# A two-block transformer kernel: the 107 KB scratch arena is allocated after the small constant tensors instead of before them

## The chip, the cores and the metric

The kernel runs on one core of one Trainium2 chip. The time is that of the device in microseconds (us), lower is better. On-chip memory (SBUF) has 128 partitions; a tensor of shape [128, n] takes 4n bytes at the same byte address of each partition when its elements are 32 bits wide. All the addresses below are such addresses inside a partition. They are those of the built program, not something the profile shows.

## The reference

Two blocks run one after the other on 512 tokens of width 1024, all in float32.

```python
def reference(x, ...):
    x = first_block(x, ...)     # DEPTH = 2 layers: w_in, differential attention, gated linear
                                # recurrence (chunk_scan, forward and backward), merge, SwiGLU
    return second_block(x, ...) # 1 layer: sliding-window attention, S5 state space, gated merge,
                                # squared-relu feed-forward

for layer in range(DEPTH):                       # first_block
    h = rmsnorm(x, attn_norm[layer])
    proj = h @ w_in[layer]
    y_a = diff_attention(...) @ w_a[layer]
    y_b = hgrn2_bidirectional(...) @ w_b[layer]
    merged = sigmoid(gate_a) * y_a + sigmoid(gate_b) * y_b
    x = x + merged @ w_o[layer]
    h = rmsnorm(x, ffn_norm[layer])
    x = x + (silu(h @ w_gate[layer]) * (h @ w_up[layer])) @ w_down[layer]
```

## The kernel before

The activations are held transposed in `xT` (feature on the partition, token along it). Every large product is made of three matmuls, because each operand is split into a high part of type fp32r and the remainder: `triple` (lines 355 to 358) multiplies high by high, high by low and low by high into the same accumulator. The weights come in units of 1 MB: the sync engine (SP) loads one into one of the two halves of `raw` (L343), ScalarE (ACT) rounds it into `w_hi` (L349), GpSimd (POOL) subtracts it into `w_lo` (L2652), and TensorE (PE) multiplies. All of this passes in a ring of two halves, guarded by semaphores that are written out by hand. There is no scheduler and no planner: each engine runs its instructions in the order of the code, and waits on semaphores.

A unit is used in one of two ways. In most stages (`pe_feature`, `pe_branch`, `pe_part`) the 128 x 128 weight tile is stationary and a row of 512 tokens of the activation moves: `h_hi`, `o_hi`, `m_hi`, `hid_hi`, `zz_hi` and their low parts. In `pe_token` and in the last product of the second block a 128 x 128 piece of the activation is stationary and 512 columns of the weight move. In the profile's names of a matmul the moving operand stands first: `psG<-hid_hi,w_hi` moves `hid_hi` over a stationary `w_hi`.

The memory of a partition is laid out once, at the top of `build_in`. Tensors made by `sb(...)` are given the next free address, each start rounded up to a multiple of 32 bytes. First come `xT`, `h_hi`, `h_lo`, `raw`, `w_hi` and `w_lo`, 16 KB each. Then comes a block of 107 KB called `arena`, which no instruction uses under its own name. Its start is kept in `base`, and some 90 tensors are placed inside it by hand with `at(name, kb, shape)`, at `base + kb * KB`; several of them share the same bytes at different times. Most intermediate results are there: `x_tok` (the input rows as loaded), `QQ`, `Kf`, `Kb`, `Tx`, `k_mix`, `prob`, `wT`, `o_hi`, `m_hi`, `hid_hi`, `rms`, the tables `Win`, `rot`, `Toep`, `Wy` and `bias` of the second block, and `y2t` and `x2t`, from which the result is stored. Some tensors of the second block lie over `h_hi` and `h_lo` instead (`o2_hi`, `yg`, `gain_row`, the tables while they are built); these do not depend on `base`. After the arena come twenty-one small tensors, 4384 bytes in all with their rounding: the identity `ident`, `ones`, `one_hot`, the per-feature gains `par` and `cur`, the masks, the rope tables, `small`, `stat`, and so on.

Line 154 is the whole of the placement:

```python
return nc.alloc_sbuf_tensor_at(name, shape, dt, offset=base + int(kb * KB))
```

Of the kernel before, what the change touches and what calls it, by code (L numbers as in the profile page):

```python
# [25 lines left out]
P = 128  # L26
# [47 lines left out]
KB = 1024  # L74
# [29 lines left out]
def build_kernel(nc, io):  # L104
    with ExitStack() as ctx:  # L105
        build_in(nc, io, ctx)


def build_in(nc, io, ctx):
    def sb(name, shape, dt=F32):  # L110
        return ctx.enter_context(nc.sbuf_tensor(name, shape, dt))
# [10 lines left out]
    raw = sb("raw", [P, 2, UNIT])  # L122
    w_hi = sb("w_hi", [P, 2, UNIT], F32R)
    w_lo = sb("w_lo", [P, 2, UNIT], F32R)
    ARENA = 107 * KB
    base = nc.sbuf_base
    sb("arena", [P, ARENA // 4])

    ident = sb("ident", [P, P])
    ones = sb("ones", [P, 2])  # L130
    one_hot = sb("one_hot", [P, 4 * HEADS])
# [15 lines left out]
    eye16 = sb("eye16", [P, GC])  # L147
    sink = sb("sink", [P, QH])
    st2 = sb("st2", [P, 6, 4])

    def at(name, kb, shape, dt=F32):
        n = 4 * int(np.prod(shape[1:])) if dt != U8 else int(np.prod(shape[1:]))
        assert kb * KB + n <= ARENA, name
        return nc.alloc_sbuf_tensor_at(name, shape, dt, offset=base + int(kb * KB))
# [2558 lines left out]
```

## Time and profile before

| | |
|---|---|
| Median of 3 runs | 2440.3 us |
| The three runs | 2435.86, 2440.3, 2440.42 us |
| Profiled execution, its own time | 2435.86 us |
| Its span, first to last instruction | 2433.9 us |
| Mean granted TensorE clock | 0.988 |
| PE busy | 2363.8 us (97% of the span) |
| PE weight load busy | 1909.8 us (78%) |
| DVE (VectorE) busy | 1247.6 us (51%) |
| POOL busy | 865.8 us (36%) |
| ACT busy | 831.3 us (34%) |
| DMA, mean over the span | 90 GB/s |

PE is the engine without slack: in 36 of the 40 slices of the span it is busy for nine tenths or more, and for a group of instructions the profile gives the mean duration of one. Matmuls overlap their neighbours, so a duration of 389 ns does not mean one matmul in 389 ns; how often one starts is read from start times, or from how many fall in a stretch.

### The profile page before, as it was taken

The page shows a single profiled execution, that of the slowest core. Times are in us where ns is not written, and L with a number is a line of the kernel's source. Part 1 is how long each engine was busy: PE and PEld are TensorE (multiplying, and loading weights), DVE is VectorE, ACT ScalarE, POOL GpSimd, SP SyncE. Part 2 cuts the span into 40 slices and gives each one's busy share as a digit, 9 for nine tenths or more (in the row PEclk, how much of TensorE's full clock was granted, in tenths as well). Part 3 has the DMA queues.
Part 4 walks back from the last instruction along what each step waited for, and adds up shares of the span by engine and source line. Part 5 has one row for each costly group of instructions (what it writes and reads, how often), then busy time and mean ns, then how long its engine had stood idle before and what let it go on. Part 6 is the DMA issues. An engine that isn't in the chain of part 4 may idle for free.

```text
span 2433.9 us, 28070 instructions
## 1 busy us (share of the span) xinstructions
PE 2363.8 (97%) x11085; PEld 1909.8 (78%) x11085; DVE 1247.6 (51%) x1561; ACT 831.3 (34%) x953; POOL 865.8 (36%) x202
## 2 busy tenths in 40 slices
PE   6998999999999999989999999999999999999998
PEld 5887766888888788877667888888888767788887
DVE  5676344564346654664445544468646652740433
ACT  4333334332222232333343422222325533422332
POOL 3332132344344343321223444444432324343433
PEclk9999999999999999999999999999999999999999
DMA  5332132344445444321333444445783324334452
GB/s 130 87 73 62 35 70 52 87 100 90 103 92 121 129 114 91 70 53 35 70 66 73 104 88 102 96 102 129 173 160 71 70 53 92 81 86 102 88 112 70
DMA packets 192727, 218.03 MB, mean 90 GB/s; under 512 B 14576, under 2 KB 165240, under 8 KB 191864
## 3 DMA queue, kind: packets, MB, share of 16 engines
q1 hardware_dynamic: 192632, 216.68, 40.7%
q8 instruction: 70, 1.15, 0.2%
q14 instruction: 25, 0.20, 0.0%
HBM read 206.92 MB, written 9.73 MB: 89 GB/s over the span
## 4 chain that ended last, share of the span: by engine, by line
issue 70%; POOL 15%; PE 13%; POOLq 0%; DVE 0%; DVEq 0%
POOL w_lo L2652 15%; PE psG L356 4%; PE psG L358 4%; PE psG L357 4%; DVE x2t L2623 0%; POOLq L2649 0%; PE psH L2131 0%; POOLq L2651 0%; DVE y2t L2633 0%; DVEq L2620 0%; PE psH L2118 0%; DVEq L2636 0%; DVEq L105 0%; DVE r4c L2619 0%; POOL ident L853 0%
## 5 line engine op out<-in xcount | busy, mean ns | idle before, releaser
L2652 POOL TENSOR_TENSOR w_lo<-raw,w_hi 128x2048 fp32r<-128x2048 f32 x186 | 859.0, 4618 | 1548.8 <-ACT w_hi L349 1544.1
L356 PE MATMUL psG<-h_hi,w_hi 128*128 128x512 f32 x1640 | 650.5, 397 | 9.1 <-DVE h_lo L487 7.8
L357 PE MATMUL psG<-h_lo,w_hi 128*128 128x512 f32 x1640 | 642.1, 392 | 0.0
L358 PE MATMUL psG<-h_hi,w_lo 128*128 128x512 f32 x1640 | 641.4, 391 | 0.0
L349 ACT CAST w_hi<-raw 128x2048 fp32r<-128x2048 f32 x185 | 353.0, 1908 | 833.6 <-PE psG L358 797.6
L356 PEld LDWEIGHTS psG<-h_hi,w_hi 128*128 128x128 f32 x1640 | 309.7, 189 | 108.7 <-issue 43.0
L358 PEld LDWEIGHTS psG<-h_hi,w_lo 128*128 128x128 f32 x1640 | 309.9, 189 | 65.7
L357 PEld LDWEIGHTS psG<-h_lo,w_hi 128*128 128x128 f32 x1640 | 309.8, 189 | 64.2 <-issue 1.4
L2591 DVE TENSOR_TENSOR hq<-r 128x512 f32<-128x512 f32 x32 | 84.9, 2692 | 148.8 <-ACT r L2357 148.8
L356 PE MATMUL psG<-hid_hi,w_hi 128*128 128x512 f32 x352 | 139.0, 395 | 1.4 <-POOL w_lo L2652 1.4
L357 PE MATMUL psG<-hid_lo,w_hi 128*128 128x512 f32 x352 | 137.7, 391 | 0.0
L358 PE MATMUL psG<-hid_hi,w_lo 128*128 128x512 f32 x352 | 137.7, 391 | 0.0
L1358 DVE TENSOR_TENSOR hid_lo<-ht,hid_hi 128x512 f32 x44 | 113.7, 2623 | 41.8 <-ACT hid_hi L1201 41.8
L356 PE MATMUL psG<-w_hi,h_hi 128*128 128x512 f32 (+1 forms) x320 | 123.2, 385 | 0.0
L358 PE MATMUL psG<-w_hi,h_lo 128*128 128x512 f32 (+1 forms) x320 | 121.2, 379 | 0.0
L357 PE MATMUL psG<-w_lo,h_hi 128*128 128x512 f32 (+1 forms) x320 | 121.2, 379 | 0.0
L796 DVE TENSOR_REDUCE stat<-psH 128x1 f32<-128x512 f32 x64 | 41.2, 686 | 141.7 <-PE psH L741 141.7
L356 PE MATMUL psG<-w_hi,hid_hi 128*128 128x512 f32 x256 | 99.9, 390 | 0.0
L358 PE MATMUL psG<-w_hi,hid_lo 128*128 128x512 f32 x256 | 99.6, 389 | 0.0
L357 PE MATMUL psG<-w_lo,hid_hi 128*128 128x512 f32 x256 | 99.6, 389 | 0.0
L1353 DVE TENSOR_TENSOR ht<-ht,psG 128x512 f32<-128x512 f32 x44 | 30.3, 688 | 130.2 <-PE psG L358 129.9
L356 PEld LDWEIGHTS psG<-hid_hi,w_hi 128*128 128x128 f32 x352 | 66.7, 189 | 16.3 <-POOL w_lo L2652 2.2
(447 smaller groups left out, 3329.2 us busy)
## 6 DMA issues: line engine op xcount, KB each, us to landing
raw<-in_w_in_dram SPq DMA_DIRECT2D x122, 512.0 KB, 6.4
raw<-in_w_gate_dram SPq DMA_DIRECT2D x44, 512.0 KB, 5.8
raw<-in_w_up_dram SPq DMA_DIRECT2D x44, 512.0 KB, 6.2
raw<-in_w_down_dram SPq DMA_DIRECT2D x32, 512.0 KB, 6.3
raw<-in_w_ff_in_dram SPq DMA_DIRECT2D x32, 512.0 KB, 6.1
raw<-in_w_ff_out_dram SPq DMA_DIRECT2D x32, 512.0 KB, 6.5
raw<-in_w_o_dram SPq DMA_DIRECT2D x16, 512.0 KB, 5.5
raw<-in_w_down_dram SPq DMA_DIRECT2D x16, 384.0 KB, 5.3
```

What stands on the lines that cost most here:

```text
L349: act.copy(w_hi[:, s, :], raw[:, s, :]).then_inc(hi_done.sem, 1)
L356: pe.matmul(out, a_hi, b_hi, start=first, stop=False)
L357: pe.matmul(out, a_hi, b_lo, start=False, stop=False)
L358: return pe.matmul(out, a_lo, b_hi, start=False, stop=last)
L796: dve.tensor_reduce(stat[:, it % 2, c:c + 1], psH[:, c, :], AX.X, ALU.max, negate=True).then_inc(sc_max.sem, 1)
L1353: mm = dve.tensor_tensor(ht[:, j, :], ht[:, j, :], psG[:, 2 + j, :], ALU.mult)\
L1358: dve.tensor_tensor(hid_lo[:, ds(i * 2 + j, 1), :].rearrange("p a t -> p (a t)"), ht[:, j, :], hid_hi[:, ds(i * 2 + j, 1), :].bitcast(F32) ...
L2591: tt(hq2[:, j, :], r2[:, j, :], r2[:, j, :], ALU.mult).then_inc(f2_q.sem, 1)
L2652: pool.tensor_tensor(w_lo[:, s, :], raw[:, s, :], w_hi[:, s, :].bitcast(F32), ALU.subtract)\
```

## The change

The three lines that reserve the arena and read its start move down, behind the last of the small tensors. Nothing else is edited.

```diff
@@ -122,10 +122,6 @@
     raw = sb("raw", [P, 2, UNIT])
     w_hi = sb("w_hi", [P, 2, UNIT], F32R)
     w_lo = sb("w_lo", [P, 2, UNIT], F32R)
-    ARENA = 107 * KB
-    base = nc.sbuf_base
-    sb("arena", [P, ARENA // 4])
-
     ident = sb("ident", [P, P])
     ones = sb("ones", [P, 2])
     one_hot = sb("one_hot", [P, 4 * HEADS])
@@ -147,6 +143,10 @@
     eye16 = sb("eye16", [P, GC])
     sink = sb("sink", [P, QH])
     st2 = sb("st2", [P, 6, 4])
+
+    ARENA = 107 * KB
+    base = nc.sbuf_base
+    sb("arena", [P, ARENA // 4])
```

The five engines have the same instructions in the same order before and after, with the same waits. What differs is addresses:

| Tensors | Byte address before | After | Shift | Start modulo 64, before and after |
|---|---|---|---|---|
| `xT`, `h_hi`, `h_lo`, `raw`, `w_hi`, `w_lo` | 16512 to 114816 | the same | 0 | 0, 0 |
| the arena and all that `at` places in it | 114816 to 224384 | 119200 to 228768 | +4384 | 0, 32 |
| `ident` | 224384 | 114816 | -109568 | 0, 0 |
| the other small tensors | 224896 to 228768 | 115328 to 119200 | -109568 | each as it was |

4384 is 17 x 256 + 32, and 137 x 32, and 274 x 16. Modulo 256 the arena's start goes from 128 to 160. 109568 is 107 KB, a multiple of 256, so each small tensor keeps its place modulo 256.

## Rows read from the trace of the kernel before

**Rows 1.** The page: span, and busy time of PE.

```profile
span 2433.9 us, 28070 instructions
PE 2363.8 (97%) x11085; PEld 1909.8 (78%) x11085; DVE 1247.6 (51%) x1561; ACT 831.3 (34%) x953; POOL 865.8 (36%) x202
```

**Rows 2.** Waits of PE: engine, line, whom it waited for, total us, times, longest.

```profile
PE psH L649 <- DVE s_diag L635: 9.6, 2, 4.8
PE psG L356 <- DVE h_lo L487: 7.8, 3, 3.9
PE psG L895 <- DMA x_tok<-in_x_dram: 7.4, 1, 7.4
```

**Rows 3.** Groups by shape: count, busy us, mean ns, idle before.

```profile
L357 PE MATMUL psG<-hid_lo,w_hi 128*128 128x512 f32 x352 | 137.7, 391 | 0.0
L357 PE MATMUL psG<-w_lo,hid_hi 128*128 128x512 f32 x256 | 99.6, 389 | 0.0
L357 PE MATMUL psG<-m_lo,w_hi 128*128 128x512 f32 x192 | 74.7, 389 | 0.0
L357 PE MATMUL psG<-o_lo,w_hi 128*128 128x512 f32 x160 | 62.9, 393 | 0.0
L357 PE MATMUL psG<-zz_lo,w_hi 128*128 128x512 f32 x32 | 13.3, 414 | 0.0
```

**Rows 4.** Busy us and count, engine by engine, clock, DMA: three full stretches.

```profile
540.00:580.00 40.00, 40.00 (x178) 33.13 (x177) 16.69 (x16) 9.46 (x10) 16.42 (x4) 1.00 0.46 97
860.00:900.00 40.00, 40.00 (x178) 33.15 (x177) 21.16 (x16) 11.65 (x10) 18.48 (x4) 1.00 0.45 99
2360.00:2400.00 40.00, 40.00 (x178) 33.13 (x177) 9.88 (x9) 10.10 (x12) 18.51 (x4) 1.00 0.45 92
```

**Rows 5.** Timeline, PE: start us, duration us; first and last of 24.

```profile
2414.65 0.39 PE L357 MATMUL psG<-w_lo,hid_hi 128*128 128x512 f32 x1
...
2419.86 0.39 PE L356 MATMUL psG<-w_hi,hid_hi 128*128 128x512 f32 x1
```

**Rows 6.** Weight loads of L357, 1700 to 1790 us: ns min/median/max.

```profile
L357 PEld LDWEIGHTS psG<-hid_lo,w_hi x56: 187/188/189, 1700.6 to 1739.3; 128*128 128x128 f32 x56
L357 PEld LDWEIGHTS psG<-w_lo,h_hi x32: 308/309/311, 1739.9 to 1764.3; 128*128 128x128 f32 x32
```

**Rows 7.** L624 alone, one stretch a level: PE and weight-load busy us, count.

```profile
97.00:102.00 5.00, 3.81 (x32) 3.65 (x32) 1.00 0.39 84
112.00:118.00 6.00, 5.49 (x32) 5.18 (x31) 1.00 0.00 0
143.00:148.00 5.00, 3.81 (x32) 3.65 (x32) 1.00 0.01 3
157.00:163.00 6.00, 3.73 (x32) 3.73 (x32) 1.00 0.00 0
172.00:177.00 5.00, 3.73 (x32) 3.73 (x32) 1.00 0.01 2
```

**Rows 8.** Instructions on tile `hre`, DVE: ns min/median/max.

```profile
L2418 DVE TENSOR_TENSOR hre<-hre,s_tmp x1: 1209/1209/1209, 1800.5 to 1800.5; 128x1008 f32<-128x1008 f32 x1
L2431 DVE TENSOR_TENSOR hre<-hre,s_tmp x1: 1226/1226/1226, 1811.2 to 1811.2; 128x1024 f32<-128x1024 f32 x1
```

**Rows 9.** DMA issues: count, KB each, median us to landing.

```profile
x_tok<-in_x_dram SPq DMA_DIRECT2D x4, 512.0 KB, 8.5
out_dram<-x2t SPq DMA_DIRECT2D x8, 256.0 KB, 2.0
t_up<-t_dram SPq DMA_DIRECT2D x1, 1024.0 KB, 6.3
rot<-rot_d SPq DMA_DIRECT2D x1, 1024.0 KB, 11.3
Wy<-wt_d SPq DMA_DIRECT2D x1, 2048.0 KB, 11.2
```

**Rows 10.** Timeline at the start: the input's loads, the first and last tile.

```profile
5.55 2.05 SPq L873 DMA_DIRECT2D x_tok<-in_x_dram  x4
18.19 0.42 PEld L895 LDWEIGHTS psG<-ident,x_tok 128*128 128x128 f32 x4 [0.27 <-DMA x_tok<-in_x_dram]
```

**Rows 11.** Instructions on tile `Wy`: its issue and its first use.

```profile
L2023 PEld LDWEIGHTS psH<-Wy,hre x64: 129/133/133, 1829.6 to 1835.9; 64*64 64x64 f32 x64
L1869 SPq DMA_DIRECT2D Wy<-wt_d x1: 325/325/325, 1795.6 to 1795.6; - x1
```

**Rows 12.** POOL, instructions of lines 2652 and 2657.

```profile
L2652 POOL TENSOR_TENSOR w_lo<-raw,w_hi x186: 4504/4605/5643, 14.0 to 2405.8; 128x2048 fp32r<-128x2048 f32 x186
L2657 POOL TENSOR_TENSOR yg<-y2t,gain_row x4: 1266/1297/1301, 2418.3 to 2427.4; 128x512 f32<-128x512 f32 x4
```

## The prediction, made before the changed kernel was run

> **What bounds the kernel now.** I read the busy times first. PE is busy for 2363.8 of 2433.9 us [rows 1], so about 70 us of the span are left in which it does nothing. The waits of PE come next: the longest sums are 9.6, 7.8 and 7.4 us, each in two or three places [rows 2]. So no wait is worth much, and what a matmul costs is worth nearly everything. Three full stretches of 40 us show that cost: 178 matmuls stand in each, whether `h_hi` from below the arena moves (540 us), mostly `hid_hi` from the arena moves (860 us), or `hid_hi` from the arena is stationary (2360 us) [rows 4]. The exact step comes from start times: 24 matmuls from 2414.65 to 2419.86 us are 23 steps of 0.2265 us [rows 5]. The granted clock is 1.00 there, its 2.4 GHz level, at which 512 columns take 213.3 ns. So 13.2 ns of a step are not columns.
>
> **The change part by part.** No instruction, wait or transfer is added, removed or reordered. The arena moves up by 4384 bytes, the small tensors move down by 107 KB. What can change is only how long an access takes at its new address, or whom it disturbs there.
>
> *The small tensors* keep their place modulo 256. They are gains, identity, masks and scalars. I cost their move at 0. If a far address mattered, `ident` at 224 KB would be the place to see it, and the groups that use the arena from its bottom to its top have the same matmul mean within 4 ns of the streaming ones: 391, 389, 389 and 393 ns [rows 3]. (`zz` with 414 ns is a short stage with starts and stops.)
>
> *The matmuls with an arena operand.* Moving from the arena: `hid` 352, `m` 192, `o` 128 of the 160 (the other 32 read `o2_hi`, which lies over `h_hi`) and `zz` 32, each three times by `triple` [rows 3]: 704 x 3 = 2112. Stationary from the arena: 256 x 3 = 768. Their start goes from 0 to 32 modulo 64. A moving row of 2048 bytes then touches, at any piece size up to 64 bytes, at most one piece more than before. What a further piece costs can be read from L624, where the moving operand hops between two tensors. In pieces of one element (112 us) 32 instructions are busy for 5.49 us, against 3.81 us for unbroken rows (97 us): 1.68 us over 32 x 128 hops, 0.41 ns a hop [rows 7]. In pieces of 16 bytes (143 us) they take 3.81 us, the same as unbroken. In pieces of 32 bytes (157 us), of which every other one starts at 32 modulo 64, they take 3.73 us, and in aligned pieces of 64 bytes (172 us) 3.73 us as well [rows 7]. So a start at 32 modulo 64 has no price there. One piece more for each of 2112 matmuls would be 2112 x 0.41 = 0.9 us, the upper end of this term; the lower end is 0, since nothing is taken away. I take 0, as the 32-byte row is the nearest. A stationary load takes 188 ns of a step of 226.5 [rows 5, 6], so it has 38 ns to spare, and is costed at 0.
>
> The Trainium skill has the matching rule, in "SBUF — State Buffer", Specifications (TRN2): SBUF is read in lines of 16 bytes, at full rate when at least two accesses hit a line. The trace agrees that the size is near that: stationary loads that step by 16 bytes take 309 ns and contiguous ones 188 [rows 6]. 4384 is 274 x 16, so by this rule no line is cut anew and the sum is exactly 0; a line of 64 bytes, which neither page nor row asserts, is what the slow rival below needs.
>
> *VectorE and ScalarE.* The clearest row for a stream that is out of step is L2418: its rows start 4 bytes past a multiple of 64 and it takes 1209 ns for 1008 elements. L2431 does the same addition on aligned rows, 1226 ns for 1024 [rows 8]. That is 1.20 ns an element both times. So VectorE pays nothing for a shift by 4 bytes, and I cost one by 32 bytes at 0. ScalarE has no such row; it is busy for 34% [rows 1], and a few ns on each of its instructions lie beside PE.
>
> *GpSimd.* The 186 subtractions into `w_lo`, 4.6 us each, work on `raw`, `w_hi` and `w_lo`, which stay where they are. Four instructions of 1.3 us read `y2t` in the arena, near the end [rows 12]. Between 0 and a doubling of the last one, this is 0 to 1.3 us; I take 0, since the other two operands stay.
>
> *DMA.* Weights go to `raw`, which stays. Of the tables that land in the arena `Wy` has the least time in hand: issued at 1795.6, landed 11.2 us later at 1806.8, first used at 1829.6 us, 22.8 us later [rows 9, 11]. Only two transfers have no cover: the input rows at the start, for which PE waits [rows 2, 10], and the last store of 2.0 us. The nearest row for an odd start is `t_up`, whose source rows start at every multiple of 4 bytes: 1 MB in 6.3 us, while `rot`, which starts at multiples of 64, needs 11.3 us for as much [rows 9]. So what sets a landing is what else is under way, not the start. I take 0; the upper end is the rival below.
>
> The page that speaks against the change is "DMA: Bandwidth & Descriptors", How a descriptor splits into AXI transactions: a piece that does not start on 256 bytes also fetches what lies before it. By its table a row of 4096 bytes costs 132 beats from 128 and 133 from 160, which would be, as an estimate, 8.5 us / 132 = 0.06 us at the start and less at the end. No run here shows beats. The sum by that page would be 0.1 us higher.
>
> The sum is 2435.86 us (the profiled execution's own time) + 0, with bounds of 0 and 0.9 + 1.3 = 2.2 us. The profiled execution is the quickest of the three; their median, 2440.3, lies 4.4 us above it, which is 0.18%. I forecast for the median: **2440 us**. A difference of 0.2%, 4.9 us, is about what a measurement of this kernel can tell from no change.
>
> **The rivals.**
>
> *A. The moving operand is fetched in aligned pieces of 64 bytes, and an access that straddles two pays for both, all along the row (slower).* The place is the 2112 matmuls that move an arena row. For it: no matmul of before moves an unbroken row that starts off 64, so this is not excluded by a row; the 64-byte pieces of L624 were all aligned. Against it: 32-byte pieces cost no more than 64-byte ones, and VectorE's shifted stream is free. Price: 32 pieces x 0.41 ns = 13 ns a matmul, 2112 x 13.1 ns = 28 us, so 2468 us. It decides from 4.9 us / 2112 = 2.3 ns a matmul on, a step of 228.8 in place of 226.5 ns.
>
> *B. Writes into the arena by DMA take twice as long (slower).* It would show where the input lands: issued from 5.55 us on, the last tile is in use at 18.19 us [rows 10], so 12.6 us become 25 and the end moves to 2453 us. Against it: the row of `t_up`, though that has odd addresses at the source only. Under 39% more landing time it stays within 4.9 us.
>
> *C. The two streams of PE stop disturbing each other (faster).* Before, the stationary and the moving operand both start at 128 modulo 256. If the 13.2 ns of a step that are not columns came from that, 2112 + 768 matmuls would lose them: 38 us, 2402 us. Against it: L624 has operands at many mutual distances inside `QQ` and `k_mix` and its later levels all take 3.73 us [rows 7], and the three stretches hold 178 matmuls each although the tensors lie at quite different distances [rows 4].
>
> *D. The change does not do what it says,* that is, the addresses stay. They do not, by the built program, but the time would be 2440 us too.
>
> **How the numbers follow.** No change, with D in it: 0.80. A: 0.06. B: 0.03. Something slower that no row shows, ScalarE or many small terms that add up to over 4.9 us: 0.03. C: 0.03. A gain of unknown origin, or one that only the spread of the runs makes: 0.05. So faster 0.08, same 0.80, slower 0.12. The likeliest case holds 2435.4 to 2445.2 us. The range of 8 in 10 adds the spread between runs of another day or chip on both sides and the small ends of the unknown costs: 2432 to 2449 us. A, B and C lie outside of it and make up 0.12.
>
> **What would show it.** Right: the means of rows 3 within 1 ns; 178 matmuls in the same stretches of 40 us, with a step of 226.5 ns for `hid_hi` and `h_hi` alike; L624 level by level as before; `x_tok` landing in about 8.5 us and PE's first tile of it near 13 us; nine tenths busy in the same slices. A shows as a longer step for moving arena rows alone, while 540 us keeps its 178. B shows as a wait of PE on `x_tok` well over 7.4 us. C shows as a step under 226 ns in the stages of `hid`, `m` and `o`. Wrong would be a difference of over 4.9 us that is in every run: if PE's groups are unchanged then, the time must be in its waits, and the engine named there is the one whose arena accesses became dear.

## The result and the profile after

The kernel is slower, by more than the range allowed. The median of five runs is 2451.72 us (2449.58 to 2456.47), against 2440.3 us for five runs of the kernel before on the same chip (2435.86 to 2441.87). The ratio is 1.0054, with a 95% interval of 1.0037 to 1.007. Forecast were 2440 us and a range of 2432 to 2449. The profiled execution took 2451.43 us, 15.6 us more than the profiled execution of before, which was the quickest of its five; the medians are 11.4 us apart.

The page, with PE's row:

```profile
span 2449.5 us, 28070 instructions
PE 2380.7 (97%) x11085; PEld 1908.6 (78%) x11085; DVE 1241.9 (51%) x1561; ACT 831.6 (34%) x953; POOL 866.4 (35%) x202
```

Beside [rows 1] the number of matmuls is the same and PE is busy for 16.9 us more (2380.7 against 2363.8). Its idle time falls a little, from 70.1 to 68.8 us. So the loss is not in waits. The waits of PE show that too (line, whom it waited for, total us, times, longest):

```profile
PE psH L649 <- DVE s_diag L635: 9.6, 2, 4.8
PE psG L356 <- DVE h_lo L487: 9.3, 3, 3.9
PE psG L895 <- DMA x_tok<-in_x_dram: 7.5, 2, 7.1
...
PE psH L1530 <- ACTq L1577: 4.3, 1, 4.3
```

The first and the third are those of [rows 2], within 0.1 us; the second is 1.5 us longer, and the last was 5.6 us before. One wait is new, 1.0 us on `Et` at L1550, and the others changed by 1.4 us or less. The groups by shape (count, busy us, mean ns) show where the time went:

```profile
L357 PE MATMUL psG<-h_lo,w_hi 128*128 128x512 f32 x1640 | 642.0, 391 | 0.0
L357 PE MATMUL psG<-hid_lo,w_hi 128*128 128x512 f32 x352 | 139.5, 396 | 0.0
L357 PE MATMUL psG<-w_lo,hid_hi 128*128 128x512 f32 x256 | 101.2, 395 | 0.0
L357 PE MATMUL psG<-m_lo,w_hi 128*128 128x512 f32 x192 | 75.8, 395 | 0.0
L357 PE MATMUL psG<-o_lo,w_hi 128*128 128x512 f32 x160 | 63.7, 398 | 0.0
```

Against [rows 3] every long group with an operand in the arena has grown by 5 or 6 ns (391, 389, 389 and 393 before), whether that operand moves (`hid_lo`, `m_lo`, `o_lo`) or is the stationary one (`hid_hi` under `w_lo`); only `zz`, 32 matmuls in a short stage, grew by 2 (414 to 416). The group without one stands at 391 ns (392 before). A mean like this is the duration of one matmul; matmuls overlap, so the exact loss is in the step from start to start. The same three stretches as in [rows 4] give it by counting:

```profile
540.00:580.00 40.00, 40.00 (x178) 33.13 (x177) 17.87 (x16) 11.54 (x12) 18.45 (x4) 1.00 0.40 85
860.00:900.00 40.00, 40.00 (x173) 32.20 (x173) 19.60 (x17) 13.59 (x13) 17.33 (x4) 1.00 0.45 96
2360.00:2400.00 40.00, 40.00 (x174) 32.17 (x173) 5.78 (x8) 9.37 (x10) 15.34 (x4) 1.00 0.53 118
```

With `h_hi` moving (540 us) 178 matmuls still fit; with `hid_hi` moving (860 us) 173 do, with `hid_hi` stationary (2360 us) 174. The granted clock is 1.00 in all three. The timeline of a full stretch, which answers to [rows 5] (start us, duration us; the first and the last of 28 matmuls):

```profile
2429.61 0.40 PE L358 MATMUL psG<-w_hi,hid_lo 128*128 128x512 f32 x1
...
2435.91 0.40 PE L358 MATMUL psG<-w_hi,hid_lo 128*128 128x512 f32 x1
```

27 steps in 6.30 us are 233.3 ns, against 226.5 before. Below, a step is the mean distance from a matmul's start to the next start, taken over those under 245 ns; it is worked out from the start times of the trace and stands in no view. By it `hid` moving goes from 226.88 to 233.34 ns, `m` from 226.88 to 233.30 and `hid` stationary from 226.81 to 233.30: 6.5 ns each. `h_hi` moving stays (227.14 and 227.16).

The other engines and the transfers answer to [rows 8, 9, 12] almost unchanged:

```profile
L2418 DVE TENSOR_TENSOR hre<-hre,s_tmp x1: 1208/1208/1208, 1809.3 to 1809.3; 128x1008 f32<-128x1008 f32 x1
L2431 DVE TENSOR_TENSOR hre<-hre,s_tmp x1: 1226/1226/1226, 1820.0 to 1820.0; 128x1024 f32<-128x1024 f32 x1
```

```profile
x_tok<-in_x_dram SPq DMA_DIRECT2D x4, 512.0 KB, 8.3
out_dram<-x2t SPq DMA_DIRECT2D x8, 256.0 KB, 2.0
t_up<-t_dram SPq DMA_DIRECT2D x1, 1024.0 KB, 6.4
```

### The profile page after: what moved, and what is told of

Same layout as the page of the kernel before. It is cut to its first block, busy times and chain, and to the rows that moved or that the text cites. A ratio compares the mean times of both kernels' runs of the same rounds, so it can differ in the third digit from the quotient of the medians.

```text
span 2449.5 us, 28070 instructions
## 1 busy us (share of the span) xinstructions
PE 2380.7 (97%) x11085; PEld 1908.6 (78%) x11085; DVE 1241.9 (51%) x1561; ACT 831.6 (34%) x953; POOL 866.4 (35%) x202
## 4 chain that ended last, share of the span: by engine, by line
issue 70%; POOL 15%; PE 13%; POOLq 0%; DVE 0%; DVEq 0%
POOL w_lo L2652 15%; PE psG L356 4%; PE psG L358 4%; PE psG L357 4%; DVE x2t L2623 0%; POOLq L2649 0%; PE psH L2131 0%; POOLq L2651 0%; DVE y2t L2633 0%; DVEq L2620 0%; PE psH L2118 0%; DVEq L2636 0%; DVEq L105 0%; DVE r4c L2619 0%; POOL ident L853 0%
## 5 line engine op out<-in xcount | busy, mean ns | idle before, releaser
L357 PE MATMUL psG<-h_lo,w_hi 128*128 128x512 f32 x1640 | 642.0, 391 | 0.0
L357 PEld LDWEIGHTS psG<-h_lo,w_hi 128*128 128x128 f32 x1640 | 310.1, 189 | 64.6 <-issue 1.5
L357 PE MATMUL psG<-hid_lo,w_hi 128*128 128x512 f32 x352 | 139.5, 396 | 0.0
L357 PE MATMUL psG<-w_lo,h_hi 128*128 128x512 f32 (+1 forms) x320 | 121.2, 379 | 0.0
L357 PE MATMUL psG<-w_lo,hid_hi 128*128 128x512 f32 x256 | 101.2, 395 | 0.0
L356 PEld LDWEIGHTS psG<-hid_hi,w_hi 128*128 128x128 f32 x352 | 66.4, 189 | 16.4 <-issue 0.5
```

Source lines behind the costliest of these rows:

```text
L356: pe.matmul(out, a_hi, b_hi, start=first, stop=False)
L357: pe.matmul(out, a_hi, b_lo, start=False, stop=False)
```

## The experiments

The expectations weigh three theories: the cost hangs on an operand's own alignment to 64 bytes (1), on where the two operands of a matmul start relative to each other, modulo 64 (2, 2a) or 256 (2b), or on something else, the order or the distance of the tensors, the small ones, another engine (3). One number sorts the runs. D is the start of the moving operand minus the start of the stationary one, modulo 256 bytes. Before, both start at 128 modulo 256, so D is 0. (One short stage, L1960, loads every fourth element of `h_hi` from starts 0, 4, 8 and 12 bytes further on; it stands apart.) After, D is 32 where the arena moves and 224 where it is stationary. In the variants, "+32" is one line, `sb("gap", [P, 8])`, at the place named.

**A bench for the step alone.** Chains of equal matmuls run over operands placed at chosen bytes; all other work of the kernel is left out, all operands hold zeros, and zeros are stored. In this bench and the two later ones the step is the mean from the ninth start of a chain to its last.

```python
MOVING = {"a": 0, "b": 4, "c": 16, "d": 32, "e": 48, "f": 64, "g": 128}
STAT = {"a": 0, "c": 16, "d": 32, "e": 48}
...
mm = pe.matmul(ps[:, 0, :], stat, move, start=i == 0, stop=i == n - 1)   # 128 times, fp32r, 512 columns
```

> Not the kernel but a bench of single matmuls; its output is zeros. On PE alone, chains of 128 fp32r matmuls (128 x 128 stationary, 512 columns moving) run one after the other, each chain with its own pair of tensors: moving operand starting at 0, 4, 16, 32, 48, 64 or 128 bytes past a multiple of 256 (mv_a to mv_g), stationary operand at 0, 16, 32 or 48 bytes past one (st_a, st_c, st_d, st_e). Then four chains of 32 plain fp32 matmuls at 0 and 32. Aligned pairs should step by 226.5 ns. Theory 1 (alignment): a matmul pays about 6.7 ns whenever one of its own operands starts off a multiple of 64, so mv_d with st_a, mv_a with st_d and mv_d with st_d all step by about 233 ns, and mv_f and mv_g with st_a by 226.5. Theory 2 (phase): what costs is that the two operands start at different places modulo 64; mv_d with st_d steps by 226.5 ns like mv_a with st_a, and mv_a with st_d by 233. Both expect the fp32 chains to be the same at 0 and 32. If no pair differs, the cost is not of PE's operands alone but of what runs beside it (theory 3).

The groups, where one kind runs back to back, so that busy us by count is near the step:

```profile
L69 PE MATMUL ps<-mv_a,st_d 128*128 128x512 f32 x128 | 30.0, 396 | 0.0
L69 PE MATMUL ps<-mv_d,st_a 128*128 128x512 f32 x128 | 30.0, 395 | 0.0
L69 PE MATMUL ps<-mv_f,st_a 128*128 128x512 f32 x128 | 29.5, 392 | 0.0
L69 PE MATMUL ps<-mv_d,st_d 128*128 128x512 f32 x128 | 29.2, 390 | 0.0
L69 PE MATMUL ps<-mv_c,st_e 128*128 128x512 f32 x128 | 29.2, 389 | 0.0
L69 PE MATMUL ps<-fm_a,fs_a 128*128 128x512 f32 x64 | 27.6, 592 | 0.0
L69 PE MATMUL ps<-fm_d,fs_a 128*128 128x512 f32 x64 | 27.6, 592 | 0.0
```

By starts, both operands aligned take 226.68 ns, either one of them at 32 takes 233.3, and both at 32 take 226.66. So an operand at 32 costs nothing by itself; a start unlike that of the other costs 6.7 ns. That speaks against alignment (theory 1) and for the distance of the two (theory 2). A moving operand at 64 took 228.9 ns and one at 128 took 232.4, where both theories had 226.5. Pairs with a start off 32 follow neither theory: stationary at 16 under moving at 0, and stationary at 48 under moving at 16 or 32, take 226.7 ns although the starts differ; all others take 228.3 to 236.7, with the moving operand at 4 the slowest (235.2 and more). The plain fp32 chains (`fm`, `fs`, two passes each) take 429.16 ns at all four combinations.

**The arena moved on by 32 bytes more (D = 64).** It starts at 192 modulo 256, a multiple of 64.

```diff
+    sb("gap", [P, 8])
     ARENA = 107 * KB
```

> The changed kernel with 32 bytes left free before the arena, which then starts at 0 modulo 64 again (192 modulo 256), 4416 bytes above its place in the kernel before; the small tensors still lie in front of it. Theories 1 and 2: the whole loss is of the 32 bytes, so the time of the kernel before, 2440 us, ratio 1.000, and a step of 226.5 ns for hid_hi. Theory 3 (the loss comes from the order, the distance of 4 KB or the new place of the small tensors): 2452 us, ratio 1.005.

2446.97 us, ratio 1.0037 (1.0024 to 1.005): not recovered, though every operand is aligned to 64 bytes. In its profile:

```profile
860.00:900.00 40.00, 40.00 (x177) 32.88 (x176) 20.11 (x17) 14.18 (x14) 17.64 (x5) 1.00 0.45 99
2360.00:2400.00 40.00, 40.00 (x173) 32.27 (x173) 8.07 (x6) 9.69 (x12) 18.54 (x4) 1.00 0.42 99
```

With the arena moving the step is 228.99 ns, with it stationary 233.34: the bench's value for 64, and, as it turned out below, for 192. The expectation of both theories failed; a rule modulo 64 is dead.

**Everything moved by 32 bytes (D = 0, all operands at 32 modulo 64).** The line stands ahead of `xT` in the kernel before.

> The kernel before with 32 bytes left free in front of everything, so that xT, h, raw, w_hi, w_lo, the arena and the small tensors all start 32 bytes later, the large ones at 32 modulo 64. Theory 1 (alignment of the operand itself): all 9,900 fp32r matmuls pay 6.7 ns, 66 us, 2506 us, ratio 1.027. Theory 2 (phase between the two operands): all pairs are in phase as before, 2440 us, ratio 1.000.

2438.53 us, ratio 1.001 (1.0001 to 1.002): at most 0.2% is left, and what the 1.4 us are was not looked for.

```profile
860.00:900.00 40.00, 40.00 (x179) 33.12 (x178) 21.34 (x16) 11.67 (x10) 18.48 (x4) 1.00 0.48 98
```

179 matmuls stand in the stretch. A start at 32 in place of 0 modulo 64 has no price here that shows in a step; theory 1, which had 2506 us, falls. (Its 9,900 matmuls were a miscount. The profile lists 8,904 of this kind, 8,808 of them with 512 columns, which makes 2500 us and changes nothing.)

**Only `w_hi` and what follows moved by 32 bytes.** The line stands between `raw` and `w_hi` in the kernel before. Now `w_hi`, `w_lo` and the arena agree with each other, and `h_hi` and `h_lo` differ from them.

> The kernel before with 32 bytes left free between raw and w_hi: w_hi, w_lo, the arena and the small tensors start 32 bytes later; xT, h_hi, h_lo and raw stay. Theory 1: every fp32r matmul has at least one operand off 64, 66 us, 2506 us, ratio 1.027. Theory 2: only the about 5,980 matmuls that pair h (or what lies over it) with a weight are out of phase, 40 us, 2480 us, ratio 1.016, while those of hid, m and o step by 226.5 ns.

2474.12 us, ratio 1.0156 (1.0139 to 1.0173), where 1.016 was expected.

```profile
540.00:580.00 40.00, 40.00 (x174) 32.17 (x173) 19.09 (x18) 12.16 (x13) 15.40 (x4) 1.00 0.48 103
860.00:900.00 40.00, 40.00 (x179) 33.11 (x178) 15.13 (x13) 12.38 (x11) 17.17 (x4) 1.00 0.53 125
```

The two stretches have changed places: `h_hi` moving is slow (233.29 ns) and the arena is back at 226.9. The cost goes with the pair, not with a tensor.

**The bench in steps of 32 bytes.** The moving operand starts at 0 to 544, the stationary one at 0, 32, 64, 128 or 256; chains of 96.

```python
MOVING = {chr(97 + i): 32 * i for i in range(18)}
STAT = {"a": 0, "b": 32, "c": 64, "e": 128, "i": 256}
```

> Again a bench of single fp32r matmuls (128 x 128 stationary, 512 columns moving), its output is zeros. 37 chains of 96; all tensors begin at a multiple of 512 plus a stated number of bytes: moving mv_a to mv_r at 0, 32, 64 and so on up to 544; stationary st_a at 0, st_b 32, st_c 64, st_e 128, st_i 256. The first 18 chains take st_a with each moving tensor, then st_b, st_c and st_e with the moving tensor that lies 0, 32, 64, 128 and 256 bytes further, then st_i with mv_a, mv_i, mv_e and mv_m. Theory 2a (phase modulo 64): 226.7 ns for every even step of 32 (0, 64, 128, ...) and 233.3 for every odd one. Theory 2b (phase modulo 256): 226.7 ns only where the two starts differ by 0 or 256 or 512, and 228 to 234 ns at all others, whatever the stationary start is. Theory 1 (the start of one operand alone) would make the pairs of st_b with mv_b and of st_c with mv_c slow.

Rows by tile (ns min/median/max, first and last start us); the last start less the first, by 95, is near the step:

```profile
L71 PE MATMUL ps<-mv_b,st_a x96: 393/396/399, 128.5 to 150.6; 128*128 128x512 f32 x96
L71 PE MATMUL ps<-mv_c,st_a x96: 388/392/398, 150.9 to 172.6; 128*128 128x512 f32 x96
L71 PE MATMUL ps<-mv_e,st_a x96: 392/394/398, 195.3 to 217.4; 128*128 128x512 f32 x96
L71 PE MATMUL ps<-mv_h,st_a x96: 389/395/398, 262.5 to 284.7; 128*128 128x512 f32 x96
L71 PE MATMUL ps<-mv_i,st_a x96: 389/389/395, 284.9 to 306.5; 128*128 128x512 f32 x96
L71 PE MATMUL ps<-mv_b,st_b x96: 387/389/398, 507.3 to 528.9; 128*128 128x512 f32 x96
```

| D | 0 | 32 | 64 | 96 | 128 | 160 | 192 | 224 | 256 |
|---|---|---|---|---|---|---|---|---|---|
| step, ns | 226.67 | 233.33 | 228.89 | 233.33 | 233.38 | 234.28 | 233.36 | 233.34 | 226.67 |

It repeats: 288 as 32, 320 as 64, 512 as 0. A stationary operand at 32, 64 or 128, tried with D = 0, 32, 64, 128 and 256, and one at 256, tried with multiples of 128, give the same values for the same D, except at D = 128: there the starts 32, 64 and 128 give 232.3 ns, as the first bench did (232.4), so D alone does not fix that value. For starts on 32 bytes the period is 256 bytes, no D is quicker than 0, and before stood on it.

**The arena at D = 0 again, in the new order.** `sb("gap", [P, 56])`, 224 bytes, ahead of the arena, which then lies 18 x 256 bytes above its old place.

> The changed kernel with 224 bytes left free before the arena: it starts 4608 bytes, 18 x 256, above its place in the kernel before, so at the same place modulo 256 as there, while the small tensors stay in front of it. Theory 2b: every matmul is as before, a step of 226.6 ns for hid, 2437 to 2440 us, ratio 1.000. Theory 3 (order of the tensors, distance, the new place of the small ones): 1.004 to 1.005. Theory 2a also expects 1.000, but has already failed to explain the kernel with a gap of 32 bytes.

2439.19 us, ratio 1.0004 (0.9995 to 1.0014): the loss is gone, as far as the interval tells. Steps of `hid` are 226.86 moving and 226.80 stationary.

```profile
860.00:900.00 40.00, 40.00 (x178) 33.10 (x178) 20.39 (x17) 13.22 (x12) 17.84 (x5) 1.00 0.45 99
2360.00:2400.00 40.00, 40.00 (x179) 33.11 (x178) 9.88 (x9) 10.02 (x12) 15.19 (x4) 1.00 0.47 103
```

**The arena on a multiple of 256 (D = 128).** `sb("gap", [P, 24])`. This is the best-aligned arena of all.

> The changed kernel with 96 bytes left free before the arena: it starts 4480 bytes, 17 x 256 + 128, above its place before, so on a multiple of 256 and by itself better aligned than ever, but 128 bytes out of step with the weights and h. Theory 2b: the bench had 232.4 ns at this distance, so the 2,880 arena matmuls lose 5.7 in place of 6.7 ns and the kernel 0.85 of what the change cost, 10 to 12 us, ratio 1.004 to 1.005. Theory 2a and theory 1: aligned to 64, so 1.000.

2454.02 us, ratio 1.0061 (1.0045 to 1.0078): 16.7 us, where 10 to 12 were expected. Steps 232.57 (`hid` moving), 233.03 (`m`) and 232.36 (`hid` stationary).

```profile
860.00:900.00 40.00, 40.00 (x174) 32.49 (x173) 19.66 (x17) 14.47 (x14) 17.14 (x5) 1.00 0.46 99
```

**The old order with the arena 32 bytes on (D = 32).** The line stands ahead of `ARENA` in the kernel before; the small tensors stay behind the arena and move on by the same 32 bytes.

> The kernel before, in its own order, with 32 bytes left free before the arena: arena and small tensors start 32 bytes later and nothing else moves. Theories 2a, 2b and 1: the same loss as the change, a step of about 233.3 ns for hid, m, o and 11 to 14 us, ratio 1.005. Theory 3 (order or the distance of 4 KB): 1.000.

2452.15 us, ratio 1.0056 (1.0039 to 1.0072), steps 233.35, 233.28 and 233.30 ns.

```profile
860.00:900.00 40.00, 40.00 (x174) 32.23 (x173) 19.62 (x17) 14.18 (x14) 16.98 (x5) 1.00 0.45 99
```

32 bytes alone make the whole effect of the change, within the intervals (1.0039 to 1.0072 against 1.0037 to 1.007). The new order without them (D = 0 above) makes at most 0.14%. Theory 3, the order, the distance or the small tensors, falls.

**Other types and widths.** The bench once more, with D = 0, 32, 64, 128, 160 and 224 for bf16, plain fp32 and 256 columns of fp32r, and with both operands at the same odd start.

```python
for n in PHASES: chain(bs, bm[n])                  # bf16
for n in PHASES: chain(fs, fm[n], 32)              # fp32
for n in PHASES: chain(rs, rm[n], cols=256)        # fp32r, half as long
for n in SAME:   mm = chain(es[n], em[n])          # both at 4, 8, 16, 24, 48
```

> A bench of single matmuls, its output is zeros. Stationary 128 x 128 starting at 0 modulo 256, moving operand at 0, 32, 64, 128, 160 and 224 (letters a, b, c, e, f, h): first bf16 with 512 columns (bs, bm), then plain fp32 with 512 columns (fs, fm), then fp32r with 256 columns (rs, rm). Last, fp32r with 512 columns where both operands start at the same 4, 8, 16, 24 or 48 bytes past a multiple of 256 (es, em with p, q, r, t, u). If the loss is a collision of two streams that are both near the rate of the memory (theory 2b), plain fp32, whose columns come at half the rate a pass (429 ns for 512 columns in the first bench), stays at 429 ns at every distance; bf16, whose elements are half as wide, loses less than fp32r or nothing; fp32r with 256 columns, where a load of about 188 ns no longer fits beside the moving operand, is set by the load and may lose more. If instead the distance costs by itself, all three lose 1 to 3%. The pairs at the same odd start: 226.7 ns if only the distance counts; above 228 if an unaligned start costs too, as two pairs of the first bench suggest (231.1 and 230.0 at 16 and 48).

```profile
L73 PE MATMUL ps<-fm_h,fs_a 128*128 128x512 f32 x64 | 27.6, 592 | 0.0
L73 PE MATMUL ps<-bm_b,bs_a 128*128 128x512 bf16 x94 | 20.8, 379 | 0.1
L73 PE MATMUL ps<-bm_h,bs_a 128*128 128x512 bf16 x94 | 20.8, 379 | 0.1
L73 PE MATMUL ps<-rm_a,rs_a 128*128 128x256 f32 x96 | 12.1, 287 | 0.0
L73 PE MATMUL ps<-rm_b,rs_a 128*128 128x256 f32 x96 | 11.5, 280 | 0.0
L73 PE MATMUL ps<-em_p,es_p 128*128 128x512 f32 x96 | 23.0, 399 | 0.0
```

Plain fp32 takes 429.16 ns and bf16 most often 215 or 216 at every D. With 256 columns the sign turns: 120 ns at D = 0 and 117.8 to 118.7 elsewhere, where a larger loss had been thought possible. Both at the same odd start is not free: 237.8 ns at 4, 231.1 at 8, 16 and 48 (the first bench had 230.0 at 48), 233.3 at 24. So "only the difference counts" holds for starts on 32 bytes alone. These types and widths were timed on zeros, in the bench alone; only fp32r with 512 columns was timed in the kernel as well, and there its steps agree with the bench.

**Kernel against bench.** The steps of the bench, times the counts, against the medians of the comparisons (the kernel before had 2437.1 to 2437.3 us in these):

| Arena, D moving / stationary | Matmuls by extra step | Worked out, us | Measured, us |
|---|---|---|---|
| old order +32: 32 / 224 | 2880 x 6.67 | 19.2 | 14.9 |
| 64 / 192 | 2112 x 2.22 + 768 x 6.69 | 9.8 | 9.8 |
| 128 / 128 | 2880 x 5.7 to 6.7 | 16.4 to 19.3 | 16.7 |
| `w_hi` moved: pairs of `h_hi`, `h_lo` and `o2` | 5880 x 6.67 | 39.2 | 37.0 |
| new order, 0 / 0 | 0 | 0 | 1.9 |
| all +32, 0 / 0 | 0 | 0 | 1.4 |

The 2880 are the count of the prediction. It left out `z`, whose 48 matmuls also move from the arena and slow down (229 to 233 ns), 0.3 us more. The 5880 hold 96 of L1960, whose step rose by 1.4 ns alone (235.2 to 236.6), 0.5 us less.

For the change itself the ratio's interval is 9.0 to 17.1 us over 2440.3, below the 19.2 us worked out. The two profiled executions, paired matmul by matmul, say where: `hid` stationary lost 4.95 us, `hid` moving 4.23, `m` 2.69, `o` 2.45, together 14.3 us, where their steps alone are 2880 x 6.5 = 18.7. Part of the difference came back where PE waits for another engine: 1.3 us at L1530 (5.6 to 4.3 us), of which the new wait at L1550 took most again, and 0.4 to 1.0 us at single starts in `hid` and `m`. That PE came later and so waited less fits it, but was not tried apart. Of the 1.3 us that are left to 15.6, 2.6 stand at matmuls with `h_hi`, whose own step did not change: 1.6 are one longer wait for `h_lo` near 30 us, and 1.2 are six more matmuls, near 2083 us, at a granted clock of 0.50. The matmuls into `psH` gave 1.2 back.

At that clock, TensorE's 1.2 GHz level, the price does not show. In the run with `w_hi` moved, `h_hi` moving at D = 224 is slow at 1.00 (233.3 ns), but these rows are 8 steps of 0.426 us:

```profile
2101.22 0.63 PE L358 MATMUL psG<-h_lo,w_hi 128*128 128x512 f32 x1
...
2104.63 0.63 PE L357 MATMUL psG<-h_hi,w_hi 128*128 128x512 f32 x1
```

Over all stretches at 0.50 of that run, 34 steps with `h_hi` or `h_lo` moving have a mean of 426.65 ns, and 32 of the kernel before, at D = 0, 426.66 ns.

## Why the prediction was wrong

**The step that failed** is *the matmuls with an arena operand*, costed at 0 with 0.9 us as its upper end. It measured 6.5 ns on each of 2880, 14.3 us net. It failed in three places.

First, "So a start at 32 modulo 64 has no price there" was read from L624 [rows 7]. There it is true, and L624 after shows no price either, 3.74 us for 32 matmuls in the stretch of 32-byte pieces (3.73 before), though both its operands lie in the arena and moved together:

```profile
157.00:163.00 6.00, 3.74 (x32) 3.73 (x32) 1.00 0.07 13
```

But L624 multiplies plain fp32, and the bench shows plain fp32 with 512 columns blind to D, at 429.16 ns for all. The row was the nearest by address, and not by the kind of instruction. No row of before could show the price, since all its unbroken fp32r streams stood at D = 0; without one, rivals A and C gave the ends of this term, and 0.9 us did not.

Second, "A stationary load takes 188 ns of a step of 226.5 [rows 5, 6], so it has 38 ns to spare, and is costed at 0." The matmuls with an arena piece as the stationary operand lose as much as the others. Time to spare in the load did not protect the step, and a load's duration does not set it: the loads of 309 ns [rows 6] stood in steps of 235 ns, by the start times of their stage.

Third, the term priced what a row touches by itself, "at any piece size up to 64 bytes, at most one piece more". The runs show the price on the two starts together: with both operands at 32 modulo 64 there is none, and their distance counts modulo 256, for which the limit of 64 had no row.

By the Trainium skill, "SBUF — State Buffer", Specifications (TRN2), lines are 16 bytes, and the prediction drew from it a sum of exactly 0. That does not decide this case: 4384 is a multiple of 16 and of 32, and the step grew all the same, by 6.5 ns. The measurement goes ahead of it.

**The rivals.** A had the place and the sign, with 0.06, but not the mechanism: it wanted slow moving rows alone, by alignment to 64. The stationary side is just as slow, an arena on a multiple of 256 is slow, and with all operands off 64 the kernel is as quick as before to 0.2%. Its 13.1 ns a matmul was twice the real 6.5. C named the right relation, two streams of PE that both start at 128 modulo 256, and had its sign wrong: leaving D = 0 gave back none of the 13.2 ns of a step that are not columns, and no place measured was quicker. Its argument from [rows 4], that tensors at quite different distances show 178 matmuls each, was empty: these distances were all multiples of 256, and L624 is plain fp32. B did not happen: `x_tok` landed after 8.3 us (8.5 before). D did not happen either, or no step would have changed.

**What held.** The bound: PE's step is worth nearly everything, no wait moved by over 1.5 us. *The small tensors* at 0: new order at D = 0 is 1.0004. *VectorE*: 1208 and 1226 ns, as before. *DMA*: `x_tok`, `out_dram` and `t_up` within 0.2 us. The 0.1 us that the prediction estimated from the Trainium skill, "DMA: Bandwidth & Descriptors", How a descriptor splits into AXI transactions, is too small to be told apart, and no run here shows beats. *GpSimd*, whose four last instructions were to cost 0 to 1.3 us more and took 1 ns more each:

```profile
L2657 POOL TENSOR_TENSOR yg<-y2t,gain_row x4: 1267/1298/1302, 2433.8 to 2443.0; 128x512 f32<-128x512 f32 x4
```

Two slips beside it cost nothing: the third of the waits named, 7.4 us, stands in one place and not in two or three [rows 2], and `ident` starts at 224384 bytes, which is 219 KB.

The range took its width from these costed terms and the spread of runs; with all rows of before on one D, 0.80 for no change was too sure.

**Open.** Why 256 bytes, and why some distances cost 2.2 and most 6.7 ns, was not settled. That the weight load and the moving stream, which overlap, get in each other's way at SBUF would fit that only their distance counts, and also that the price is gone where columns pass more slowly: plain fp32, and fp32r at the 1.2 GHz level. Nothing here runs a matmul without its load, so it is not shown. The pairs of unlike starts off 32 that take 226.7 ns, and the reversed sign at 256 columns, have no account either. No version that beats the kernel before was found, since no pair of starts tried with 512 columns was quicker than 226.7 ns.

## What to carry to other kernels

Place moving and stationary fp32r operands of matmuls of 512 columns at the same byte modulo 256, on starts of 32, and look at that again whenever a tensor is inserted ahead of a block placed by hand: 32 bytes cost this kernel 0.5% on 2880 matmuls and 1.6% on 5880. For a price that the trace doesn't show, take the nearest row of the same type and shape, and if all rows share the property that the change breaks (here D = 0), their agreement says nothing on its price.

## What was not expected of the hardware

- At a granted clock of 1.00, with starts on 32 bytes, the step of back-to-back fp32r matmuls of 512 columns is 226.67 ns when both operands start alike modulo 256, 228.89 at a distance of 64, and 232.3 to 234.3 at the other multiples of 32; plain fp32 (429.16 ns) and bf16 (215 or 216) do not see it.
- At a granted clock of 0.50 the step is 426.65 ns with the operands apart and 426.66 alike.
- With 256 columns the like start is the slower one, 120 ns against 117.8 to 118.7.
- Both operands at the same start off 32 bytes cost 230.0 to 237.8 ns for 512 columns, while three pairs of unlike starts off 32 took 226.7.
